# Moving the split activations of a two-block transformer kernel to other byte remainders in SBUF

## What is computed

```python
for i in range(2):                                   # first block: two layers
    ax, ac = modulate(norm(hx)), modulate(norm(hc))
    yx, yc = mixer(ax, ac)                           # layer 0 "even", layer 1 "odd"; yc only in layer 0
    hx = hx + gx1 * yx
    hx = hx + gx2 * (relu(modulate(norm(hx)) @ w1) ** 2 @ w2)     # w1: 1024 x 4096
    if i == 0:
        hc = hc + gc1 * yc
        hc = hc + gc2 * (relu(modulate(norm(hc)) @ w1) ** 2 @ w2)
x = norm(hx)
for l in range(2):                                   # second block: two layers of projections,
    x = layer_norm(ALPHA * x + mixer_2(x, l))        # three kinds of attention, an output projection
```

## The kernel before

| tensor | first byte before | remainder before | first byte after | remainder after |
|---|---|---|---|---|
| whi, wlo | 49,280 and 65,664 | 128 | the same | 128 |
| Hh, layer 0 / layer 1 | 117,312 | 64 | 117,376 / 117,504 | 128 / 0 |
| Hl, layer 0 / layer 1 | 133,696 | 64 | 133,888 / 134,016 | 0 / 128 |
| HIDh, layer 0 / layer 1 | 181,184 | 192 | 181,632 / 181,760 | 128 / 0 |
| HIDl, layer 0 / layer 1 | 197,568 | 192 | 198,144 / 198,272 | 0 / 128 |
| Gh, Gl | 117,312 and 125,504 | 64 | 117,504 and 125,696 | 0 |
| CQh, CQl | 200,896 and 209,088 | 192 | 201,088 and 209,280 | 128 |

## Time and profile before

### The profile page before, as it was taken

One profiled execution on the slowest core, in us unless ns is written; L12 is line 12 of the kernel. 1 busy time (PEld: TensorE's weight loads), 2 busy tenths in 40 slices (PEclk: granted clock), 3 DMA queues, 4 the chain that ended last, 5 costly groups with the idle time before them and its releaser, 6 DMA issues. The chain is left out here.

```text
span 1346.4 us, 25050 instructions
## 1 busy us (share of the span) xinstructions
PE 1311.5 (97%) x9434; PEld 1156.3 (86%) x9434; DVE 988.9 (73%) x1734; ACT 668.7 (50%) x1358; POOL 195.2 (14%) x268
## 2 busy tenths in 40 slices
PE   7999999999999999999999999999999999999997
PEld 6786679988888888898896899999999988999967
DVE  5698778999887878979428665655665786865974
ACT  4427743631523414334237664565465566465573
POOL 0101213000000000123104610000220016120043
PEclk8999999999999999999999999999999999999999
DMA  8774124365985867834320245655475433454511
GB/s 300 285 214 146 49 94 152 140 226 205 316 314 197 287 242 256 303 130 156 110 79 17 77 151 167 222 182 175 151 257 172 147 130 104 159 173 172 173 49 47
DMA packets 67665, 233.15 MB, mean 173 GB/s; under 512 B 7280, under 2 KB 12400, under 8 KB 67312
## 3 DMA queue, kind: packets, MB, share of 16 engines
q1 hardware_dynamic: 67568, 231.84, 50.2%
HBM read 230.76 MB, written 1.05 MB: 172 GB/s over the span
## 5 line engine op out<-in xcount | busy, mean ns | idle before, releaser
L957 DVE TENSOR_TENSOR wlo<-raw,whi 128x1024 fp32r<-128x1024 f32 (+1 forms) x284 | 346.4, 1221 | 148.5 <-ACT whi L599 142.7
L599 ACT ACTIVATE whi<-raw 128x1024 fp32r<-128x1024 f32 (+1 forms) x284 | 296.4, 1044 | 266.1 <-PE ps L1712 264.9
L1710 PE MATMUL ps<-Hh,whi 128*128 128x256 f32 (+1 forms) x896 | 302.6, 338 | 3.6 <-DVE wlo L957 1.6
L1711 PE MATMUL ps<-Hl,whi 128*128 128x256 f32 (+1 forms) x896 | 299.2, 334 | 0.0
L1712 PE MATMUL ps<-Hh,wlo 128*128 128x256 f32 (+1 forms) x896 | 298.9, 334 | 0.0
L1710 PEld LDWEIGHTS ps<-Hh,whi 128*128 128x128 f32 x896 | 169.2, 189 | 25.9 <-issue 5.7
L1712 PEld LDWEIGHTS ps<-Hh,wlo 128*128 128x128 f32 x896 | 169.0, 189 | 18.9
L1711 PEld LDWEIGHTS ps<-Hl,whi 128*128 128x128 f32 x896 | 169.4, 189 | 18.1
L1712 PE MATMUL ps<-HIDh,wlo 128*128 128x256 f32 (+1 forms) x536 | 176.1, 329 | 0.0
L1711 PE MATMUL ps<-HIDl,whi 128*128 128x256 f32 (+1 forms) x536 | 175.9, 328 | 0.0
L1710 PE MATMUL ps<-Gh,whi 128*128 128x256 f32 x624 | 175.6, 281 | 0.1
(11 more groups left out here) (266 smaller groups left out, 2061.5 us busy)
## 6 DMA issues: line engine op xcount, KB each, us to landing
raw<-wall SPq DMA_DIRECT2D x270, 512.0 KB, 4.2
aring<-aall SPq DMA_DIRECT2D x144, 512.0 KB, 4.7
raw<-wall SPq DMA_DIRECT2D x14, 384.0 KB, 3.0
AL<-ali SPq DMA_DIRECT2D x14, 192.0 KB, 5.5
X<-xin SPq DMA_DIRECT2D x2, 1024.0 KB, 7.1
BI<-rpb SPq DMA_DIRECT2D x4, 512.0 KB, 9.9
out<-X SPq DMA_DIRECT2D x4, 256.0 KB, 2.4
cst<-const SPq DMA_DIRECT2D x1, 960.0 KB, 8.4
```

What stands on the lines that cost most here:

```text
L599: act.activation(whi[:, slot, 0:n], raw[:, slot, 0:n], ACT.Copy).then_inc(sem("w_hi"), 1)
L957: dve.tensor_tensor(wlo[:, slot, 0:n], raw[:, slot, 0:n], whi[:, slot, 0:n].bitcast(F32), ALU.subtract)\
L1710: pe.matmul(o, a[0], b[0], start=first, stop=False)
L1711: pe.matmul(o, a[0], b[1], start=False, stop=False)
```

## The change

No instruction is added, removed or moved on any engine: the order and the waits of all five are the same. What changes is where operands lie. H and HID each become one tensor of two parts, `H2` and `HID2`, of 128 bytes (`PLACE` = 32 columns) more than the 16,384 bytes that a part needs; layer 0 uses the first 16,384 bytes of a part, layer 1 the last. Three unused tensors (`place_h`, `place_hid`, `place_g`) shift what follows them. A part is 16,512 bytes long, which is 128 more than a multiple of 256, so that the low part has the other remainder than the high part in either layer. What comes after H and HID in SBUF shifts too (`Q0`, `K0`, `V0` and `BI` from remainder 192 to 0, `aring` and `SB` from 64 to 128, `AL` from 64 to 0).

```diff
+SPLIT = 2 * N * KT
+PLACE = 32
...
-        Hh = sb("Hh", [P, KT, 2 * N], F32R, b1)
-        Hl = sb("Hl", [P, KT, 2 * N], F32R, b1)
+        sb("place_h", [P, 16], F32, b1)
+        H2 = sb("H2", [P, 2, SPLIT + PLACE], F32R, b1)
...
-        HIDh = sb("HIDh", [P, KT, 2 * N], F32R, sm)
-        HIDl = sb("HIDl", [P, KT, 2 * N], F32R, sm)
+        sb("place_hid", [P, 32], F32, sm)
+        HID2 = sb("HID2", [P, 2, SPLIT + PLACE], F32R, sm)
...
         b2 = ExitStack()
+        sb("place_g", [P, 48], F32, b2)
         Gh = sb("Gh", [P, KT, N], F32R, b2)
...
+        def placed(t, layer, part):
+            c0 = PLACE * layer
+            return t[:, part, c0:c0 + SPLIT].rearrange("p (k n) -> p k n", k=KT)
+
+        Hh, Hl = ([placed(H2, layer, part) for layer in range(2)] for part in range(2))
+        HIDh, HIDl = ([placed(HID2, layer, part) for layer in range(2)] for part in range(2))
...
-            Hx = (lambda k: Hh[:, k, :], lambda k: Hl[:, k, :])
+            Hx = Hd
```

More of the change, by code:

```diff
@@ L241, in mod @@
             return lambda k: SC[:, scale_row, k:k + 1], lambda k: adacol(s, v, t0 + k)
-        Hd = (lambda k: Hh[:, k, :], lambda k: Hl[:, k, :])
-        Hdx = (lambda k: Hh[:, k, 0:N], lambda k: Hl[:, k, 0:N])
+        Hd = [(lambda k, layer=layer: Hh[layer][:, k, :], lambda k, layer=layer: Hl[layer][:, k, :]) for layer in range(2)]
+        Hdx = (lambda k: Hh[1][:, k, 0:N], lambda k: Hl[1][:, k, 0:N])
         Gd = (lambda k: Gh[:, k, :], lambda k: Gl[:, k, :])
@@ L250, in program @@
         norms = {}
-        norms["l0a"] = Norm(xt, 8, 512, D, [(0, *mod(0, 0, 0, 0)), (N, *mod(1, 0, 1, 0))], Hd,
+        norms["l0a"] = Norm(xt, 8, 512, D, [(0, *mod(0, 0, 0, 0)), (N, *mod(1, 0, 1, 0))], Hd[0],
                             ready=lambda k: [(f"x_landed{k // 4}", 16)])
-        norms["l0b"] = Norm(xt, 8, 512, D, [(0, *mod(2, 0, 0, 24)), (N, *mod(3, 0, 1, 24))], Hd,
+        norms["l0b"] = Norm(xt, 8, 512, D, [(0, *mod(2, 0, 0, 24)), (N, *mod(3, 0, 1, 24))], Hd[0],
                             ready=counted("out_added", 0))
-        norms["l1a"] = Norm(xt, 8, 512, D, [(0, *mod(4, 1, 0, 0)), (N, *mod(5, 1, 1, 0))], Hd,
+        norms["l1a"] = Norm(xt, 8, 512, D, [(0, *mod(4, 1, 0, 0)), (N, *mod(5, 1, 1, 0))], Hd[1],
                             ready=counted("mlp_added", 25))
@@ L442, in program @@
                     v=(lambda p, kt, r, h=h: V1[:, kt, P * h:P * h + P]),
-                    dst=(Hh[:, h, P * t:P * t + P], Hl[:, h, P * t:P * t + P]), diff=True))
+                    dst=(Hh[1][:, h, P * t:P * t + P], Hl[1][:, h, P * t:P * t + P]), diff=True))
         J_L1 = (J_L0[1], len(jobs))
@@ L770, in attend, with mlp @@
                         exps(s)
-            def mlp(u0, h0, T, n):
+            def mlp(layer, u0, h0, T, n):
                 def quarter(it, last=None):
@@ L784, in quarter @@
                             act.wait_ge(sem("hid_a"), 8 * it + (h0 + j + 1))
-                            act.activation(HIDh[:, j, 0:T], M[:, j % 2, 0:T], ACT.Copy).then_inc(sem("hid_h"), 1)
+                            act.activation(HIDh[layer][:, j, 0:T], M[:, j % 2, 0:T], ACT.Copy).then_inc(sem("hid_h"), 1)
                         elif last and last.pair is not None and j == 8 + HALVED:
@@ L847, in _ @@
                 hi_c(norms["l0b"], k)
-            mlp(U_L0_MLP, 0, 512, norms["l1a"])
+            mlp(0, U_L0_MLP, 0, 512, norms["l1a"])
             for i in range(L1_FM):
@@ L870, in _ @@
             his(norms["l1b"])
-            mlp(U_L1_MLP, 32, 256, norms["fin"])
+            mlp(1, U_L1_MLP, 32, 256, norms["fin"])
             his(norms["fin"])
@@ L2039, in project_out, with mlp @@
                     halves(norm, range(u0 + HALVED, u0 + KT), OUT_BANKS, x, free)
-            def mlp(u0, h0, T, ready, first=None, last=None):
+            def mlp(layer, u0, h0, T, ready, first=None, last=None):
                 def quarter(it, head=None, tail=None):
@@ L2048, in quarter @@
                         pe.wait_ge(sem("out_added"), HALVED + 2)
-                        first_stream(head, units, banks, Hx)
-                        second_stream(head, units, banks, Hx)
+                        first_stream(head, units, banks, Hx[layer])
+                        second_stream(head, units, banks, Hx[layer])
                         groups = groups[1:]
@@ L2067, in quarter @@
                             for j in group:
-                                b = ((Hh, Hl) if j < 8 else (HIDh, HIDl))
+                                b = ((Hh[layer], Hl[layer]) if j < 8 else (HIDh[layer], HIDl[layer]))
                                 bank = HID_BANKS[j % 4] if j < 8 else 2 + j % 2
@@ L2082, in quarter @@
                         halves(tail, range(u0 + 16 * it + 8 + HALVED, u0 + 16 * it + 16),
-                               MLP_BANKS, (lambda k: HIDh[:, k, :], lambda k: HIDl[:, k, :]),
+                               MLP_BANKS, (lambda k: HIDh[layer][:, k, :], lambda k: HIDl[layer][:, k, :]),
                                free)
@@ L2127, in _ @@
                     ins = mm3(ps[:, i, 0:2 * N], wtile((U_L0 + i) % SLOTS, P * k, P),
-                              (Hx[0](k), Hx[1](k)), k == 0, k == KT - 1)
+                              (Hx[0][0](k), Hx[0][1](k)), k == 0, k == KT - 1)
                     if k == KT - 1:
                         ins.then_inc(sem("w_used"), 1)
-            project(p_l0, FIRST, L0_FM, Hx)
-            values(U_L0 + L0_FM, V_L0, 4, Hx, (0,), V_L0 - 4)
+            project(p_l0, FIRST, L0_FM, Hx[0])
+            values(U_L0 + L0_FM, V_L0, 4, Hx[0], (0,), V_L0 - 4)
             pe.wait_ge(sem("proj_out"), V_L0)
@@ L2137, in _ @@
             scores(1)
-            values(U_L0 + L0_FM, V_L0, 4, Hx, (1,))
+            values(U_L0 + L0_FM, V_L0, 4, Hx[0], (1,))
             pe.wait_ge(sem("a_used"), ADA_EARLY + ADA_PROJ)
             attend(*J_L0, begun=2, values_out=V_L0 + 4)
-            project_out(U_L0_OUT, 0, 512, Hx, [("o_lo", HL[3 * k + 2]) for k in range(KT)],
+            project_out(U_L0_OUT, 0, 512, Hx[0], [("o_lo", HL[3 * k + 2]) for k in range(KT)],
                         norm=norms["l0b"])
-            mlp(U_L0_MLP, 0, 512, norms["l0b"].h0, norms["l0b"], norms["l1a"])
+            mlp(0, U_L0_MLP, 0, 512, norms["l0b"].h0, norms["l0b"], norms["l1a"])
             pe.wait_ge(sem("mlp_added"), 8 * (QUARTERS - 1) + 1 + HALVED + 2)
             pe.wait_ge(sem("added_x"), 4)
[L2148 to L2151, removed]
+            first_stream(norms["l1a"], range(U_L1, U_L1 + TOGETHER), [(p_l1.o0 + i) % 4 for i in range(TOGETHER)], Hx[1])
+            project(p_l1, TOGETHER, L1_ORDER.index(8), Hx[1])
+            project(p_l1, L1_ORDER.index(8), L1_ORDER.index(8) + 1, Hx[1], second=norms["l1a"].h0)
+            project(p_l1, L1_ORDER.index(8) + 1, L1_FM, Hx[1])
             for c in range(4):
@@ L2157, in _ @@
                     scores(J_L1[0] + 1)
-                values(U_L1 + L1_FM + 2 * c, V_L1 + 4 * c, 4, Hx, free=V_L1 + (-4, 0, 4, 12)[c])
+                values(U_L1 + L1_FM + 2 * c, V_L1 + 4 * c, 4, Hx[1], free=V_L1 + (-4, 0, 4, 12)[c])
             attend(*J_L1, begun=2, values_out=V_L1 + 16)
-            project_out(U_L1_OUT, 8, 256, Hx, [("sub_lo", 2 * k + 2) for k in range(KT - 2)] + [("late_lo", 2), ("late_lo", 4)],
+            project_out(U_L1_OUT, 8, 256, Hx[1], [("sub_lo", 2 * k + 2) for k in range(KT - 2)] + [("late_lo", 2), ("late_lo", 4)],
                         {2: J_L1[1] - 3, 4: J_L1[1] - 2, 5: J_L1[1] - 1})
@@ L2165, in _ @@
             keep(3, 6)
-            mlp(U_L1_MLP, 32, 256, norms["l1b"].h0)
+            mlp(1, U_L1_MLP, 32, 256, norms["l1b"].h0)
             sums(norms["fin"])
```

4 lines of the change are left out of this document (2 added, 2 removed).

## The result

| | us |
|---|---|
| before, 4 runs | 1342.16, 1344.54, 1346.84, 1442.13 (median 1345.69, without the last 1344.54) |
| after, median of 4 runs | 1354.14 (1353.96 to 1355.37) |
| ratio after / before | 1.0073, 95% interval 1.0059 to 1.0087 |

The changed kernel is 0.73% slower. The forecast was 1329 us, 1.3% faster. The time lies inside the stated range, but it moved the other way than forecast. One of the before runs, 1442.13, stands far from the others and is left out of the ratio.

A forecast was written before the change was run, and what follows sets the result against it. PE's streams were taken to bound the kernel; 5.5 us from 512 columns plus 12.7 us from 256 made 18.2 us, giving 1330.1 from 1348.3, or 1329 us against the median. The 8 in 10 range was 1300 to 1358.

The forecast's parts named there:

- What bounds the kernel: Whole kernel: PE, busy 1311.5 of 1346.4 us, sets the time; nearly all that its streams lose or gain reaches the end.
- I put the step down to the address: Layer 0's MLP, 512 columns: H at 233.3 ns against HID's 228.9 was explained by the moving operand's address remainder.
- 256 columns, H, G and HID: Matmuls of 256 columns: new places keep all on the fast level (113.3 ns, slow is 117.8), 12.7 us gained.
- all slow, 5.9 us lost: Lower bound of the term for 256 columns on H, G and HID: every matmul takes the slow level.
- All slow: Rival for the whole kernel: every stream takes the slow level, 9 us lost, 1356 us; chance 0.09.
- 512 columns: Wide matmuls: H goes from 233.3 to HID's 228.9 ns, 5.5 us gained; HID is there already.
- does less than its words: Rival: only one of each pair has the named remainder, 1335 to 1341 us; counted with the forecast, together 0.38.
- A step slower: Rival: Hh at the weights' remainder and remainders changing between matmuls cost 4.4 ns steps; 36 us lost, 1383; chance 0.07.
- The level holds as long as the stream runs, and a wait or a change of operand can switch it: Streams of 256 columns: the address alone does not set the level; H was 276 and 281 ns at one address.
- The rule against it: Skill's rule of independent PE read ports: no place would change the time; the no-change rival said 1347 us, chance 0.22.
- The prediction's other rule: Matmuls at full clock take N/2.4 + 2.5 ns, 215.8 and 109.2; an estimate by it would be 1287 us.
- the unhindered rival: Rival: streams come nearer to the columns alone, 76.7 us gained in whole, half of it 38 us, 1308; chance 0.24.

The follow-up runs named there:

- e9: Against the kernel before: layer 0's H and HID at remainder 128, layer 1's H and HID, G and CQ at 240; 1333.03 us against 1346.11, ratio 0.9903.
- e1: Against the kernel before: both parts alike, layer 0's H and HID and CQ at 128, layer 1's and G at 0; 1347.0 us against 1344.95, ratio 1.0022.
- e3: Against the kernel before: only the weights' high and low part moved, from remainder 128 to 192, activations unmoved; 1353.93 us against 1344.95, ratio 1.0074.
- e5: Against the kernel before: only layer 0's H and HID moved, both parts to remainder 128; 1338.24 us against 1346.86, ratio 0.9941.
- e2: Against the kernel before: only G moved to remainder 0 and CQ to 128; 1349.2 us against 1344.95, ratio 1.0036.
- e10: Against the kernel before: only H and HID moved, parts alternating as in the changed kernel, G and CQ unmoved; 1349.07 us against 1346.11, ratio 1.0026.
- e6: Against the kernel before: activations moved to odd multiples of 16 bytes upward in remainder, weights kept at 128; 1346.14 us, one time.
- e7: Against the kernel before: activations moved to odd multiples of 16 bytes downward in remainder, weights kept at 128; 1356.27 us, one time.
- e8: Against the kernel before: low weights moved from remainder 128 to 192; layer 0's H and HID, and G, at 128; 1350.82 us, one time.
- e11: Against the kernel before: activations a few bytes off remainders 128 (layer 0) and 240 (the rest), weights kept at 128; 1371.88 us, one time.

## Why the prediction was wrong

**What bounds the kernel** was right. PE's busy time rose by 8.0 us, the span of the same executions by 5.7 and the median by 9.6; in e9 PE's busy time fell by 18.3, the span by 17.2 and the median by 13.1. Nothing else came to the front. (The sentence on DVE's room rests on rows 8, not 7.)

**"I put the step down to the address"** was right. e1, e3 and e9 move addresses alone, and levels move with them.

**The step that failed** is "*256 columns, H, G and HID*": "if the place matters at all, the fast level is the one that the trace shows at either remainder." It assumed that a new place picks one of the two levels on view. It does not: a place has levels of its own, some one and some several. Remainder 0 brought 118.7 and the alternating pairs 117.8 to 120.0, all above the slow level or at it. In place of 12.7 us gained, G, H and HID lost 5.6 + 4.6 + 2.1 = 12.3 us. The bound "all slow, 5.9 us lost" was too small for the same reason, and the prediction's last sentence had named this case without giving it a price in the sum. That the time came near the 1356 of "All slow" is luck: no stream of G took the slow level 117.8, and H at 512 columns gained.

**512 columns** was mis-sized and half missed. H gained 2.3 ns rather than 4.4, and HID, "there already", lost 2.2: together 1.3 us gained instead of 5.5. The cause is what the prediction counted as its slow side under "does less than its words": only one part of each pair has the named remainder. With both parts at 128 the same streams come to 226.7, better than the forecast (e1, e5). The low part's 128 bytes cost the change some 0.5% or 7 us (ratio 1.0073 against 1.0022 in e1, which also leaves the tensors behind H and HID at their old remainders).

**"A step slower"** (Hh at the weights' own remainder costs more) was wrong in its first half at 512 columns, where the weights' remainder is the best place found (e1, e3); at 256 columns that remainder does cost, 120.0 against 117.8, half of the step that it was priced at. Its second half, alternation, is real at 512 columns against both parts at 128, 226.7 to 231.1, but smaller than priced and not the whole: e2 loses without it, and in layer 1 the pair (229.0) is faster than both parts at 0 (233.3).

**"The level holds as long as the stream runs, and a wait or a change of operand can switch it"** stays true for place 64: in e5 the stream of G from 1148.7 us is at 113.3 and that from 1301.1 at 117.8. G's mean at that place was 115.69 in before, 115.01 in e5 and 114.55 in e10, so the share of either level differs between executions.

**The rule against it.** The runs show moves of 64 bytes or less, in an otherwise equal program, that change a stream from 226.7 to 237.4 ns and from 113.3 to 121.8, and in e3 it is the distance to the weights that counts. The Trainium skill, SBUF — State Buffer, section "Who interferes with whom", gives moving reads and weight loads independent ports and says that PE never waits on anyone; by that no place would change the time, and these measurements do not agree with it for streams of this kind. The prediction's other rule was taken from the wrong case: the Trainium skill, TensorE: Matmul & The Clock Gate, section "Back-to-back issue gap", gives N/2.4 + 2.5 ns for an isolated matmul and says that in a stream of weight loads and matmuls both set the spacing. Here each matmul has a weight load ahead of it, and no settled stream came below 226.7 and 113.3 ns.

**What stays open.** That the moving read and the weight load meet inside SBUF is a guess that fits e3; no view shows it. Nor is it known why some places (16, 64, 112, 232) hold several levels and others one, what picks the level, or why the price of three matmuls is not the mean of its parts. e6, e7, e8 and e11 have one time and one trace each, so their places may hold levels that were not seen. Places were tried in steps of 16 or 32 bytes and only a few between, so a better one may exist.

## What to carry to other kernels

Where PE streams without waits, as here, the byte remainders of moving and stationary operand relative to each other are a tuning knob (here worth a per cent, e9), which costs no instruction; but the value of a place that the trace has not shown must be measured, for each width of its own, since neighbours by 4 bytes can lie at opposite ends. Put both parts of a split operand at the good place: with one of them 128 bytes off, layer 0 lost 4.4 ns a matmul. Read such a change from starts over whole slabs: durations by line show only a third of a stream, and a "fast" and a "slow" level on view are not a list of all levels.

## What the runs showed that was not expected

- Many of the means are steps of one size, counted over the three matmuls of a slab: at 512 columns 3 x 226.67 = 680.0 ns, then 686.7, 693.3 and 700.0; at 256 columns 340.0, 353.3 and 360.0. A step is 6.67 ns. Other places (32, 80, 132, 176, 244, and 0 and 96 at 256 columns) fall between. They are means only: read to the nanosecond, H of before alternates between 236 and 231 ns in layer 0's MLP, HID there goes round 226, 229 and 232, and G of the changed kernel repeats over five matmuls (120, 119, 115, 117, 122).
- The best place depends on the width: distance 0 is the best at 512 columns (226.7) and among the worse at 256 (120.0).
- No place came nearer to the prediction's columns alone than 13.3 ns at 512 columns (226.7 - 213.3) and 6.7 at 256 (113.3 - 106.7). That leaves (1,944 x 13.3 + 4,224 x 6.7) ns = 54 us of the 76.7 that the unhindered rival counted, untouched by any place tried.
